# Four split weight buffers and two raw ones, in place of two and four, in a two-layer hybrid decoder on one core

## What is computed

```python
def swiglu(x, w_in, w_out):
    a, b = jnp.split(x @ w_in, 2, axis=-1)
    return (jax.nn.silu(a) * b) @ w_out
...
    for l in range(DEPTH):                                   # 2
        h = h + 0.5 * swiglu(rmsnorm(h, ffn1_norm[l]), ffn1_w_in[l], ffn1_w_out[l])   # D_FF = 2816
        u = rmsnorm(h, mix_norm[l])
        q_a, c_kv, iq, ik, iw, z_pool, q_c, gate_pre = jnp.split(u @ w_in[l], split_pts, axis=-1)
        ...
        y_a = dsa_attention(q_a, c_kv, iq, ik, iw, w_uk[l], w_uv[l], rel_bias)   # top-128 of the indexer's score
        y_b = pool_mixer(z_pool, w_pool[l], pool_scale[l])
        y_c = mem_attention(q_c, rmsnorm(mem, mem_norm[l]), w_mem_kv[l])         # 256 memory tokens
        g = jax.nn.sigmoid(gate_pre).reshape(B, S, N_BRANCH, D)
        merged = (g[:, :, 0] * (y_a @ w_branch_a[l])
                  + g[:, :, 1] * (y_b @ w_branch_b[l])
                  + g[:, :, 2] * (y_c @ w_branch_c[l]))
        h = h + merged @ w_out[l]
        h = h + 0.5 * swiglu(rmsnorm(h, ffn2_norm[l]), ffn2_w_in[l], ffn2_w_out[l])
    return rmsnorm(h, final_norm)
```

## Time and profile before

| | |
|---|---|
| median of 3 runs | 2257.93 us |
| the profiled execution | 2256.72 us, span 2254.9 us |
| TensorE matmul busy | 2209.5 us, 98% |
| DVE / ACT / POOL busy | 963.2 / 548.4 / 1320.7 us |
| granted TensorE clock, mean | 0.996 |
| weights and all else read from HBM | 204.9 MB, 93 GB/s with what is written |

### The profile page before, as it was taken

How to read it: one execution, slowest core, us unless ns; L and a number is a source line. 1 busy time by engine, 2 the same in 40 slices (tenths; PEclk the granted TensorE clock), 3 DMA queues, 4 the chain that set the end, 5 groups by cost and what they waited for, 6 DMA issues and landing times.

```text
span 2254.9 us, 31688 instructions
## 1 busy us (share of the span) xinstructions
PE 2209.5 (98%) x10328; PEld 1813.3 (80%) x10328; DVE 963.2 (43%) x1803; ACT 548.4 (24%) x1030; POOL 1320.7 (59%) x868
## 2 busy tenths in 40 slices
PE   7999999999999999999999999999999999999996
PEld 5888888778788888888788888888778888888885
DVE  4331345478754532023433222536877454321334
ACT  3110112443553211001121101215445432100111
POOL 5666667544436666666756666675444366666663
PEclk9999999999999999999999999999999999999998
DMA  6243323221213222322323332232121132323322
GB/s 173 101 131 105 100 77 120 89 71 62 67 56 99 94 93 88 101 100 85 108 98 120 105 110 94 78 121 82 61 71 64 50 112 94 99 83 107 101 78 72
DMA packets 67524, 209.81 MB, mean 93 GB/s; under 512 B 7368, under 2 KB 10600, under 8 KB 67176
## 3 DMA queue, kind: packets, MB, share of 16 engines
q1 hardware_dynamic: 63600, 202.84, 27.4%
q10 hardware_dynamic: 3832, 5.77, 1.1%
HBM read 204.91 MB, written 3.67 MB: 93 GB/s over the span
## 4 chain that ended last, share of the span: by engine, by line
PE 93%; DVE 4%; issue 1%; ACT 1%; DMA 0%; POOL 0%; DVEq 0%; ACTq 0%; POOLq 0%
PE bank L550 29%; PE bank L552 28%; PE bank L551 28%; PE obank L790 1%; PE sbank L735 1%; PE tbank L757 1%; DVE picks L1289 1%; DVE top L1287 1%; PE obank L568 0%; PE obank L562 0%; PE sbank L727 0%; PE sbank L710 0%; PE obank L774 0%; PE sbank L688 0%; PE sbank L741 0%
## 5 line engine op out<-in xcount | busy, mean ns | idle before, releaser
L504 POOL TENSOR_TENSOR wL<-raw,wH 128x1024 fp32r<-128x1024 f32 (+3 forms) x432 | 913.9, 2116 | 36.1
L501 POOL TENSOR_SCALAR wH<-raw 128x1024 fp32r<-128x1024 f32 (+3 forms) x432 | 406.9, 942 | 872.3 <-PE bank L552 858.5
L550 PE MATMUL bank<-u0H,wH 128*128 128x512 f32 x1408 | 551.4, 392 | 6.3 <-POOL wL L504 4.1
L552 PE MATMUL bank<-u0L,wH 128*128 128x512 f32 x1408 | 548.8, 390 | 0.0
L551 PE MATMUL bank<-u0H,wL 128*128 128x512 f32 x1408 | 548.8, 390 | 0.0
L550 PEld LDWEIGHTS bank<-u0H,wH 128*128 128x128 f32 x1408 | 265.0, 188 | 64.8 <-issue 8.7
L551 PEld LDWEIGHTS bank<-u0H,wL 128*128 128x128 f32 x1408 | 264.9, 188 | 55.5 <-issue 1.0
L552 PEld LDWEIGHTS bank<-u0L,wH 128*128 128x128 f32 x1408 | 264.9, 188 | 55.2
L550 PE MATMUL bank<-u1H,wH 128*128 128x512 f32 x704 | 293.3, 417 | 4.7 <-DVE u1L L1488 2.7
L552 PE MATMUL bank<-u1L,wH 128*128 128x512 f32 x704 | 275.2, 391 | 0.0
L551 PE MATMUL bank<-u1H,wL 128*128 128x512 f32 x704 | 274.9, 390 | 0.0
(11 more groups left out here) (174 smaller groups left out, 2140.1 us busy)
## 6 DMA issues: line engine op xcount, KB each, us to landing
raw<-in_wA SPq DMA_DIRECT2D x176, 512.0 KB, 3.2
raw<-in_wM SPq DMA_DIRECT2D x96, 512.0 KB, 3.3
raw<-in_wB SPq DMA_DIRECT2D x64, 384.0 KB, 3.0
raw<-in_wB SPq DMA_DIRECT2D x64, 320.0 KB, 2.9
raw<-in_wR SPq DMA_DIRECT2D x32, 256.0 KB, 2.6
h<-in_xT ACTq DMA_DIRECT2D x4, 512.0 KB, 7.3
mem<-in_memT SPq DMA_DIRECT2D x2, 1024.0 KB, 6.9
near_bias<-bias_rows ACTq DMA_DIRECT2D x2, 1024.0 KB, 7.0
```

Of the source, the lines that this page charges most:

```text
L501: pool.tensor_scalar(wH[:, w, 0:cols], raw[:, slot, 0:cols], 1.0, 0.0, ALU.mult, ALU.add).then_inc(rounded, 1)
L504: pool.tensor_tensor(wL[:, w, 0:cols], raw[:, slot, 0:cols], wH[:, w, 0:cols].bitcast(F32), ALU.subtract).then_inc(split_done, 1)
L550: pe.matmul(dst, a, hi[:, k, :], start=first and i == 0, stop=False)
L552: mm = pe.matmul(dst, a, lo[:, k, :], start=False, stop=last and i == len(tiles) - 1)
```

## The change

The numbers of raw and split buffers are exchanged: 2 raw, 4 split. TensorE and POOL take the split buffer as the unit's number modulo 4, POOL the raw one modulo 2; the counts on which they wait follow from the two constants. Two split buffers (wH and wL) are 16 KB per partition more, two raw ones 8 KB less. The room is made by placing `mem_rms` behind `mem` in the FFN's part of SBUF and `picks2` and `picks3` in `yL[:, 3]` and `yH[:, 3]`, so that these stay free until the last query block: branch A's output of block a is now written whole into `yH[:, a]` and `yL[:, a]`, and its matmuls read it through the view `yaH`, `yaL`, in which the 512 positions of a column block k are four pieces of 128.

```diff
-RAW_SLOTS, SPLIT_SLOTS, BANKS = 4, 2, 4
+RAW_SLOTS, SPLIT_SLOTS, BANKS = 2, 4, 4
...
-assert UNITS % RAW_SLOTS == 0 and CHUNKS % BANKS == 0
+assert UNITS % SPLIT_SLOTS == 0 and CHUNKS % BANKS == 0
...
-        mem_rms = sb("mem_rms", [P, M])
...
+            mem_rms = sb("mem_rms", [P, M], F32, ffn)
...
-            picks = [None] + [sb(f"picks{b}", [P, P * (b + 1)], F32, mix) for b in range(1, QB)]
...
+            picks1 = sb("picks1", [P, 2 * P], F32, mix)
...
+        with ExitStack() as sparse:
+            sb("hole7", [P, 3 * T], F32, sparse)
+            picks3 = sb("picks3", [P, T], F32, sparse)
+            sb("hole8", [P, (KD - 4) * T], F32, sparse)
+            sb("hole9", [P, 3 * T], F32, sparse)
+            picks2 = sb("picks2", [P, 3 * P], F32, sparse)
+        picks = [None, picks1, picks2, picks3]
...
+        yaH, yaL = (t[:, 0:4, :].rearrange("p a t -> p (a t)").rearrange("p (b k t) -> p k b t", b=QB, k=4)
+                    for t in (yH, yL))
...
-            def split(l, group, unit, slot, cols):
...
-                w = slot % SPLIT_SLOTS
+            def split(l, group, unit, w, cols):
...
+                slot = w % RAW_SLOTS
...
-                    with pool.Fori(0, count // RAW_SLOTS) as j:
-                        for s in range(RAW_SLOTS):
-                            split(l, j + first // RAW_SLOTS, l * UNITS + j * RAW_SLOTS + (first + s), s, cols)
+                    with pool.Fori(0, count // SPLIT_SLOTS) as j:
+                        for s in range(SPLIT_SLOTS):
+                            split(l, j * (SPLIT_SLOTS // RAW_SLOTS) + (first + s) // RAW_SLOTS,
+                                  l * UNITS + j * SPLIT_SLOTS + (first + s), s, cols)
...
-                        split(l, j * 3 + (U_GBC + i) // RAW_SLOTS, l * UNITS + j * 12 + (U_GBC + i),
-                              (U_GBC + i) % RAW_SLOTS, 1024 if i % 3 < 2 else 512)
+                        split(l, j * (12 // RAW_SLOTS) + (U_GBC + i) // RAW_SLOTS, l * UNITS + j * 12 + (U_GBC + i),
+                              (U_GBC + i) % SPLIT_SLOTS, 1024 if i % 3 < 2 else 512)
...
-                            exact(bank[i][:, :], i % 2, [(k, k) for k in range(KD)], u0H, u0L,
+                            exact(bank[i][:, :], i, [(k, k) for k in range(KD)], u0H, u0L,
...
-                                    exact(bank[i][:, :], part_, tiles, hidH, hidL, first=part_ == 0,
+                                    exact(bank[i][:, :], (2 * i + part_) % SPLIT_SLOTS, tiles, hidH, hidL, first=part_ == 0,
...
-                    w = i % 2
+                    w = (U_MEM + i) % SPLIT_SLOTS
...
-                        exact(bank[(C_IN + cof) % BANKS][:, :], (U_IN + off) % 2,
+                        exact(bank[(C_IN + cof) % BANKS][:, :], (U_IN + off) % SPLIT_SLOTS,
...
-                        w = (U_GBC + 3 * i + 2) % 2
+                        w = (U_GBC + 3 * i + 2) % SPLIT_SLOTS
...
-                    exact(bank[(C_BA + f) % BANKS][:, :], (U_BA + f) % 2, [(k, k) for k in range(4)],
-                          yH, yL).then_inc(unit_used, 1)
+                    exact(bank[(C_BA + f) % BANKS][:, :], (U_BA + f) % SPLIT_SLOTS, [(k, k) for k in range(4)],
+                          yaH, yaL).then_inc(unit_used, 1)
...
-                    exact(bank[(C_WO + f) % BANKS][:, :], (U_WO + f) % 2, [(k, k) for k in range(KD)],
+                    exact(bank[(C_WO + f) % BANKS][:, :], (U_WO + f) % SPLIT_SLOTS, [(k, k) for k in range(KD)],
...
-                        act.activation(yH[:, 0:4, a * P:(a + 1) * P], src[:, :].rearrange("p (a t) -> p a t", t=P),
-                                       ACT.Copy).then_inc(ya_high, 1)
+                        act.activation(yH[:, a, :], src[:, :], ACT.Copy).then_inc(ya_high, 1)
...
-                        dve.tensor_tensor(yL[:, 0:4, a * P:(a + 1) * P],
-                                          src[:, :].rearrange("p (a t) -> p a t", t=P),
-                                          yH[:, 0:4, a * P:(a + 1) * P].bitcast(F32), ALU.subtract
+                        dve.tensor_tensor(yL[:, a, :], src[:, :], yH[:, a, :].bitcast(F32), ALU.subtract
```

## The result

The changed kernel takes **2264.99 us** (median of 8 runs, 2262.96 to 2267.23) against 2257.94 us for the kernel before on the same chip (8 runs, 2256.59 to 2259.09). The ratio is 1.0033, with a 95% interval of 1.0024 to 1.0042. It is slower by 7 us, where 3 us of gain were forecast, and outside the range of 2252.0 to 2258.3.

The account below looks back on a forecast made before the run. TensorE, busy 98% of the span, was taken as the bound, so only removed waits count. Terms -3.00 - 2.34 + 0.4 + 1.90 = -3.04 us took the median from 2257.93 to 2254.9, range 2252.0 to 2258.3.

Parts of the forecast that it names:

- Two raw buffers: Weight loads: each needs 3.3 us and fits behind the 3.54 us split between, so halving the raw buffers costs 0.
- Rival A: Kernel's start: loses nothing, as the third raw load comes late or DVE gets ahead; gain 4.94 us, 2253.0; 17 in 100.
- Rival D: Start: TensorE's clock falls in the longer pauses, 2.5 us lost over an assumed 5 us of work; 2257.4; 5 in 100.
- The start's +1.90: Kernel's start: POOL's third split at 17.65 blocks DVE's u0L column 6, so column 7 ends later; +1.90 us, once.
- rival B: Start: u0L column 7 is blocked too, by the fourth split, ending 2.8 us later; -0.2, 2257.7; 11 in 100.
- (a): First unit of W_out: with four split buffers TensorE's wait for POOL's split falls away; 1.50 us per layer, -3.00.
- (b): First w_in unit, after the memory units: the wait for POOL's split falls away; 1.17 us per layer, -2.34.
- Rival C: W_out: DVE does hold its first unit, as the profile names it, so nothing is gained there; 2257.9; 7 in 100.
- (c): First memory unit: starts about 0.5 us earlier per layer, but the wait for DVE's ssq grows by that; 0.
- (d): Norm chain, memory stage: DVE's L1137 waits for POOL's splits; 0.2 us per layer, +0.4 in all, bound 1.68 per layer.
- rival E: Branch A: each matmul loses something at jumps between operand pieces, so slower, 2266.4 at 60 ns each; 8 in 100.

Follow-up runs that it names:

- raw2: The kernel before with two raw buffers in place of four, two split buffers as they were: 2270.67 us, ratio 1.0056.
- light: The changed kernel, storing only 8 of the 128 copies of the bias row: 2258.31 us, ratio 1.0006.
- pieces: The changed kernel, with the bias store cut in six pieces issued in passes of ACT's first feed-forward loop: 2257.6 us, ratio 1.0008.
- pieces_before: The kernel before with only its bias store cut in six pieces and moved into the first feed-forward layer: 2257.6 us, ratio 1.0001.
- layout: The kernel before with only the placement edits of the change, four raw and two split buffers kept: 2257.57 us, ratio 1.0001.
- halves: The kernel with cut bias store and held third split, plus GpSimd's subtraction of each 1024-column unit of gates B and C in two halves: 2253.45 us, ratio 0.9984.
- pieces_hold: The changed kernel with the bias store cut in six, and POOL's third split waiting until DVE has made all of u0L: 2254.65 us, ratio 0.9986.

## Why the prediction was wrong, point by point

- **The step that failed** is "Two raw buffers": the load "needs 3.3 us", then "Hidden; if it slips, only POOL's lead of four units shrinks", priced at 0, and with it, in the start, "lands some 3.3 us later, at 17.0, ahead of 17.68". The median of steady loads was carried into the start, where a store of 1536 KB runs on 8 of the 16 DMA engines. There the load took 17.5 us, POOL had no lead yet, and TensorE lost 5.7 us, then 2.3 to the clock and 1.5 at the next late load. The trace of the kernel before held a load issued at the same time that landed at 31.0. raw2 has the loss without the four split buffers, the loss goes in light and pieces when only the store is changed, and pieces_before shows that four raw buffers hid it.
- **Rival A** (the start loses nothing) had the right premise, the third load late "(after about 21)", and concluded a gain, since DVE would be free of POOL. DVE was indeed free: its u0L steps up to 22 us stand as before. But a load at 31 is later than TensorE needs it, and the rival had no price for that.
- **Rival D**, the clock, happened, in a pause much longer than the 2.0 us it was reckoned for: 4.75 us of matmuls ran at 0.50, and cost 2.3 us where 2.5 stood. The 5 us of the rival were an assumption, so that the two agree is luck.
- **The start's +1.90** is right where its condition holds: light shows +1.79, with the three DVE durations as forecast. There rival B (the fourth split blocks column 7) did not come in either. In the changed kernel that condition, a third split at 17.65, never held, and unit 0 ended as before, which the prediction had named as a sign of being wrong.
- **(a) and (b)** were right to 0.01 us, -1.50 and -1.17 per layer, in every kernel with four split buffers that was run. Rival C (DVE holds W_out) is false: layout and raw2, with two split buffers, gain nothing there. **(c)** was right as a sum, absorbed by the ssq wait but for 0.1 us. What it left out is that a longer wait may not be free: it grew from 1.25 to 2.02 us, and behind it the clock fell in layer 1. The other traces fit, without proving it. Of ten kernels with four split buffers six show a lower clock in the memory stage of layer 2, and of four with two split buffers none does.
- **(d)** was mis-sized in one layer: 0 and +1.27 against 0.2 each, within the stated bound of 1.68. In pieces it is 0 in both, so that it depends on how the chain lies against POOL's splits.
- **Missing from the sum** was the same collision in the gates stage: +1.47 per layer, 2.9 us in all, as much as (a). The prediction looked for DVE blocks at the start and in the norm chain, and not at every DVE instruction that lies beside a GpSimd split with a wait behind it. The halves run moves this cost by changing only the length of GpSimd's instruction.
- **The Trainium skill,** "SBUF — State Buffer", section "Who interferes with whom", also names VectorE's tensor_scalar, in its two-port modes, among the instructions that share a port pair with GpSimd, where whoever issues first holds it for its whole instruction and the other is blocked. The trace agrees: 2.50 us beside a 2.39 us subtraction, 1.39 beside a half of one.
- **The layout** costs nothing: rival E (the pieces slow branch A) is false. layout reads 1.0001, and branch A's matmuls start 0.227 us apart on average there, as before.
- **The boundary's -1.34** was not foreseen. TensorE's gap there has 1.56 us of issue time before and 0.23 after. In the kernels with four split buffers it is between 0 and 0.31, in those with two between 1.56 and 1.82 (the first line below is of the kernel before):

```profile
1126.33 0.49 PE L550 MATMUL bank<-u0H,wH 128*128 128x512 f32 x1 [1.56 <-issue]
...
1133.72 0.39 PE L563 MATMUL bank<-hidL,wH 128*128 128x512 f32 x1
1134.34 0.49 PE L561 MATMUL bank<-u0H,wH 128*128 128x512 f32 x1 [0.23 <-issue]
```

  In the trace TensorE's backward branch at the end of the layer takes 3.75 us in place of 4.97; it is 3.35 to 3.87 in all ten kernels with four split buffers and 4.97 to 5.23 in the four with two, raw2 and layout among them. So it goes with the split buffers, and neither with the raw ones nor with the layout. What makes it shorter was not tried: the loops over units are unrolled differently and the code is another, so its length or its place may be the cause. This stays open.

The terms as forecast, with the missed ones in place, are +9.5 - 3.0 - 2.3 + 1.3 + 2.9 - 1.3 + 0.2 + 1.2 (lower clock at 394.7) - 0.5 (small shifts) = +8.0, the difference of the two spans. The clock term is not peculiar to the change: light, pieces_hold and layout show a similar 3.4 us stretch between 385 and 391.

## What to carry to other kernels

- A median landing time says nothing of the kernel's start. Look up the last part of each load there, on every DMA engine, beside the stores that run at the time; a prefetch depth of four can hide a load of 17 us, which only shows when the depth is cut.
- Buffers that let GpSimd run ahead also move what it does under every VectorE step. List each VectorE instruction that excludes it, with the wait behind it, in every stage; hold GpSimd back for short critical chains, or cut its instructions, rather than reorder the others.
- Where the profile names one releaser of several, check that one against the program: here DVE's ta was named at 50.55, and it was a late load.
- After adding or moving a tile, compare how many matmuls start in a quiet window. Here 64 unused bytes cost 19 us, more than the whole change.

## What the runs showed of the hardware that had not been expected

- A store of 1024 packets of 1536 bytes out of 8 partitions keeps 8 of the 16 DMA engines until 33 us after its issue, and a load on another queue that has half its parts on them lands after 17.5 us in place of 3.3.
- TensorE's pace depends on where its moving operand starts in SBUF. Tiles shifted by 16 bytes: 861 matmuls in 200 us. Shifted by 64 bytes: 877, in one kernel 868. Not shifted: 886. The operands behind the new tile slow down: the median distance for u0 and hidden is 225 to 231 ns with 64 bytes and 233 ns with 16, in place of 226. The u1 operand ahead of it keeps its 226 to 227 ns. Which addresses are good was not mapped.
- VectorE's tensor_scalar is held up by GpSimd with constants from a tile as with immediate values: 2.498 against 2.500 us.
- In a pause of TensorE from 29.4 to 34.95 us the granted clock fell to 0.50, at 32.9, and came back at 39.70. Stretches at 0.50 also come behind the ssq waits of 1.3 to 2.0 us, in some profiled executions and not in others: 3.4 us near 385 and 6.8 us at 1490.9 in pieces_hold, none in pieces. The other executions of pieces have lower mean clocks, and their times go with these.
